# A pair's dilated attention between the half chunks of the next pair's projections, all pairs written out

## The reference, cut to what matters

```
qa, ka, va = xn @ W_in (columns by group g and head)       # 3 groups of 8 heads of 64; 2048 prompt tokens, D = 1024
for (window, dil) in ((128, 1), (512, 4), (2048, 16)):     # group g; keys at distances 0, d, 2d, ..., window
    s = q . k * 64**-0.5 + alibi bias                      # blocks of 128 queries by 256 (or 128) keys
    lse = logsumexp(s);  o = exp(s - lse) @ v
win{g}_prompt = the last min(window, 2048) rows of (k, v)  # an output
win{g}_sample = state_win{g} moved on by 4 tokens          # an output: copied DRAM to DRAM
```

## Time and profile before

| | |
|---|---|
| median of 3 runs | 3882.95 us |
| the profiled execution's own time | 3883.4 us |
| its span | 3880.7 us |
| TensorE busy | 3412.9 us, 88% |
| VectorE, ScalarE busy | 1313.1 us, 952.7 us |
| dilated stage, first projection to last value matmul | 200.24 to 1630.27 us |
| mean granted TensorE clock | 0.913 of full speed |

### The profile page before, as it was taken

How to read it: one execution, slowest core, us unless ns; L and a number is a source line. 1 busy time by engine, 2 the same in 40 slices (tenths; PEclk the granted TensorE clock), 3 DMA queues, 4 the chain that set the end, 5 groups by cost and what they waited for, 6 DMA issues and landing times. The chain is left out here.

```text
span 3880.7 us, 52570 instructions
## 1 busy us (share of the span) xinstructions
PE 3412.9 (88%) x18808; PEld 2853.8 (74%) x18808; DVE 1313.1 (34%) x3549; ACT 952.7 (25%) x1838; POOL 416.7 (11%) x557
## 2 busy tenths in 40 slices
PE   3899999999998898699999997899999997239799
PEld 3877777788776686599999996566766665138787
DVE  4111222211222112222211112556656554763333
ACT  4421222211221112212122222333333332011121
POOL 0000000000000000000000002222333320013200
PEclk6999999999997887799999999899999998569899
DMA  3133322233312222232223323223333331765443
GB/s 118 50 121 116 108 82 89 91 116 120 111 57 81 88 79 76 81 99 79 81 85 86 89 69 108 92 85 109 109 108 108 108 107 44 263 201 182 165 127 114
DMA packets 351647, 407.75 MB, mean 105 GB/s; under 512 B 114154, under 2 KB 307403, under 8 KB 349483
## 3 DMA queue, kind: packets, MB, share of 16 engines
q1 hardware_dynamic: 308186, 182.18, 16.7%
q0 software_dynamic: 43280, 223.22, 16.3%
HBM read 318.14 MB, written 175.19 MB: 127 GB/s over the span
## 5 line engine op out<-in xcount | busy, mean ns | idle before, releaser
L109 PE MATMUL dil_S<-all_xT_hi,dil_w_hi 128*128 128x512 f32 x1152 | 468.4, 407 | 17.6 <-DVE dil_w_lo L621 17.6
L110 PE MATMUL dil_S<-all_xT_lo,dil_w_hi 128*128 128x512 f32 x1152 | 461.6, 401 | 0.0
L111 PE MATMUL dil_S<-all_xT_hi,dil_w_lo 128*128 128x512 f32 x1152 | 460.7, 400 | 0.0
L109 PE MATMUL gate_ps<-all_xT_hi,gate_w_hi 128*128 128x416 f32 x960 | 346.7, 361 | 13.8 <-DVE gate_w_lo L1074 13.8
L111 PE MATMUL gate_ps<-all_xT_hi,gate_w_lo 128*128 128x416 f32 x960 | 338.5, 353 | 0.0
L110 PE MATMUL gate_ps<-all_xT_lo,gate_w_hi 128*128 128x416 f32 x960 | 337.7, 352 | 0.0
L2168 PE MATMUL mla_S<-mla_k,mla_q 96*128 96x512 f32 (+3 forms) x640 | 287.5, 567 | 12.9 <-ACT mla_p L1956 7.5
L2196 PE MATMUL mla_O<-mla_v,mla_pT 128*128 128x66 f32 x2176 | 270.5, 274 | 4.6 <-DVE mla_rec L2115 4.6
L109 PEld LDWEIGHTS dil_S<-all_xT_hi,dil_w_hi 128*128 128x128 f32 x1152 | 222.3, 193 | 67.4 <-DVE dil_w_lo L621 17.7
L2196 PEld LDWEIGHTS mla_O<-mla_v,mla_pT 128*128 128x128 f32 x2176 | 262.6, 195 | 8.9 <-issue 7.2
L111 PEld LDWEIGHTS dil_S<-all_xT_hi,dil_w_lo 128*128 128x128 f32 x1152 | 220.8, 192 | 51.7
(11 more groups left out here) (269 smaller groups left out, 5435.5 us busy)
## 6 DMA issues: line engine op xcount, KB each, us to landing
out_win_sample<-in_state_win POOLq DMA_DIRECT2D x16, 4088.0 KB, 14.7
mla_kv<-in_state_win POOLq DMA_DIRECT2D x72, 512.0 KB, 12.4
scr_gates<-gate_out POOLq DMA_DIRECT2D x120, 208.0 KB, 2.2
mla_qb<-scr_hs POOLq DMA_DIRECT2D x32, 768.0 KB, 11.8
dil_raw<-in_w_in SPq DMA_DIRECT2D x36, 512.0 KB, 4.1
proj_gm<-scr_gates SPq DMA_DIRECT2D x40, 416.0 KB, 3.3
gate_ckv<-in_cache_ckv SPq DMA_DIRECT2D x256, 64.0 KB, 1.8
out_win_sample<-in_state_win POOLq DMA_DIRECT2D x4, 4064.0 KB, 2.3
```

The costliest lines, as they stand in the source:

```text
L109: pe.matmul(out, w[0], x[0], start=first, stop=False)
L110: pe.matmul(out, w[0], x[1], start=False, stop=False)
L111: return pe.matmul(out, w[1], x[0], start=False, stop=last)
```

## The change: what it does, and the diff

Time of a pair is cut into 24 slots, one for each half chunk (12 matmuls) of its projections, written out for 12 pairs and a 13th pass without projections. In pass `n`, TensorE does the half chunk of pair n, and behind it a piece of the attention of pair a = n - 1: in an even slot 2u turns(u-1) and scores(u), in an odd slot 2u+3 values(u); slots 18 to 23 hold no attention. Projections go through a PSUM tile `PJ` of two banks; `S`, `O` and `sm` have one buffer; `raw` has one buffer instead of two, and `w` goes round by weight. V and K are transposed in slots 18 to 21. `knat` is now the two halves of `sm`. `kT` has two buffers. Record buffers stay four. GpSimd's program is the same but for blank lines. Each load of a weight waits until the one before has been split (`w_lo`), and stands in slots 4, 12 and 20 of SyncE's order.

```diff
-        raw = [m.sb(f"raw{b}", [P, KC, P]) for b in range(2)]
+        NU = NT // 2
+        NP = 4 * NG
+        raw = m.sb("raw", [P, KC, P])
...
+        knat = [sm[:, b, :, :].rearrange("p h (x c) -> p (h x) c", c=P) for b in range(2)]
+        PJ = m.ps("PJ", [P, 2, 512])
+        S = m.ps("S", [P, 2, 512])
...
+        def scored(slot):
+            return slot // 2 if slot % 2 == 0 and slot < 2 * NU else None
+        def turned(slot):
+            return slot // 2 - 1 if slot % 2 == 0 and 2 <= slot <= 2 * NU else None
+        def valued(slot):
+            return (slot - 3) // 2 if slot % 2 == 1 and 3 <= slot < 2 * NU + 3 else None
...
+                def load(p):
+                    n, o = divmod(p, 3)
+                    if p:
+                        sp.wait_ge(w_lo, p)
...
+                for n in range(NP + 1):
+                    for slot in range(SLOTS):
+                        if n < NP:
+                            p = n * 3 + slot // 8 + 2
+                            if slot % 8 == 4 and p < 3 * NP:
+                                load(p)
+                            if slot == 16:
+                                sp.wait_ge(masked, n * NU)
...
+                            if slot in (6, 14):
+                                store_sample(n, slot // 8)
+                            if TURN_FROM < slot <= TURN_FROM + KN[n // 4]:
+                                store_keys(n, slot - TURN_FROM - 1)
+                            if slot == SLOTS - 1:
+                                store_values(n)
+                                store_sample(n, 2)
+                        if n and valued(slot - 1) is not None:
+                            store_records(n - 1, valued(slot - 1))
...
+                        if n and scored(slot - 1) is not None:
+                            exps(n - 1, scored(slot - 1))
+                        if n and turned(slot) is not None:
+                            turn_out(n - 1, turned(slot))
...
+                        p = n * 3 + slot // 8 + 1
+                        if slot % 8 == 3 and 1 < p < 3 * NP:
+                            high(p)
...
-                        held(dve, rec_stored[u % 4], (n * (NU // 4) + u // 4) * 32, dve_ticks)
...
+                    if u == 0:
+                        dve.wait_ge(bias_in, a * 16 + 16)
+                        for b in range(2):
+                            dve.wait_ge(kn_stored[b], 16 * ((KN_BASE[a + 1] + 1 - b) // 2))
+                    if c > 3:
+                        dve.wait_ge(rec_stored[u % 4], c // 4 * 32)
...
+                        if n and turned(slot) is not None:
+                            turn_out(n - 1, turned(slot))
+                        if n and scored(slot) is not None:
+                            mask(n - 1, scored(slot))
+                        if n and valued(slot) is not None:
+                            record(n - 1, valued(slot))
...
+                for n in range(NP + 1):
+                    for slot in range(SLOTS):
+                        if n < NP:
+                            project(n, slot)
+                            if slot in (4, 12):
+                                sample(n, slot // 8)
...
+                        if n:
+                            if turned(slot) is not None:
+                                turns(n - 1, turned(slot))
+                            if scored(slot) is not None:
+                                scores(n - 1, scored(slot))
+                            if valued(slot) is not None:
+                                values(n - 1, valued(slot))
```

More of the change, by code:

```diff
@@ L425, in stage_dilated @@
         kn_ready, kn_out = m.sem("kn_ready"), m.sem("kn_out")
-        kn_stored = [m.sem("kn_stored_sm"), m.sem("kn_stored_raw")]
+        kn_stored = [m.sem(f"kn_stored{b}") for b in range(2)]
         v_stored, hs_stored = m.sem("v_stored"), m.sem("hs_stored")
@@ L431, in stage_dilated @@
         rec_stored = [m.sem(f"rec_stored{b}") for b in range(4)]
-        sp_ticks, dve_ticks = m.sem("sp_ticks"), m.sem("dve_ticks")
-        NU = NT // 2
         KN_TILES = [min(w_, SEQ) // P for w_, _ in GROUPS]
         KN = [-(-n // 4) for n in KN_TILES]
[L436 to L458, removed]
+        KN_BASE = [sum(KN[i // 4] for i in range(n)) for n in range(NP + 1)]
+        ORDER = (2, 1, 0)
+        READY = (vT_ready, k_ready, q_ready)
+        OUT = (vT_out, k_out, q_out)
+        SLOTS = 24
+        TURN_FROM = 18
         def blocks(g, u):
@@ L499, in body @@
                             .then_inc(v_stored, 16)
[L500 to L527, removed]
+                def store_keys(n, k):
+                    g, hp = divmod(n, 4)
+                    i = KN_BASE[n] + k
+                    tiles = min(4, KN_TILES[g])
+                    rows = slice(k * 4 * P, (k * 4 + tiles) * P)
+                    sp.wait_ge(kn_out, i + 1)
+                    sp.dma_start(t[f"win{g}_prompt"][0][rows, 0, hp * P:(hp + 1) * P].rearrange("(s p) c -> p s c", p=P),
+                                 knat[i % 2][:, 0:tiles, :]).then_inc(kn_stored[i % 2], 16)
@@ L570, in _ @@
[L570 to L612, removed]
@@ new lines, in _ @@
+                low(0)
+                low(1)
+                for n in range(NP + 1):
+                    for slot in range(SLOTS):
+                        if n and turned(slot) is not None:
[4 more added lines that the diff above has]
+                            record(n - 1, valued(slot))
+                        if n == NP:
+                            continue
+                        if slot % 2 and slot // 8 == 1:
+                            empty(n, slot % 8 // 2)
+                        if TURN_FROM <= slot < TURN_FROM + KN[n // 4]:
+                            lay_keys(n, slot - TURN_FROM)
+                        p = n * 3 + slot // 8 + 1
+                        if slot % 8 == 3 and 1 < p < 3 * NP:
+                            low(p)
@@ L796, in sample, with project @@
-                def sample(n, o):
-                    which, b = ORDER[o]
-                    if o == 0:
-                        waits(pe, rec_out, n * NU)
-                    out = O[0:NS, 0, :, :].rearrange("p a b -> p (a b)")[:, which * P:(which + 1) * P]
+                def project(n, slot):
+                    o, k, half = slot // 8, slot % 8 // 2, slot % 2
+                    p = n * 3 + o
+                    if k == 0 and half == 0:
+                        pe.wait_ge(w_lo, p + 1)
+                    if half == 0 and (n or slot > 2):
+                        n1, s1 = (n, slot - 4) if slot >= 4 else (n - 1, slot + SLOTS - 4)
+                        pe.wait_ge(OUT[s1 // 8], n1 * 4 + s1 % 8 // 2 + 1)
+                    for c in range(4 * half, 4 * half + 4):
+                        last = split_matmul(pe, PJ[:, k % 2, :], [w_hi_t[p % 2][:, c, :], w_lo_t[p % 2][:, c, :]],
+                                            [xT[x][:, c, k * 512:(k + 1) * 512] for x in range(2)], c == 0, c == KC - 1)
+                    if half:
+                        last.then_inc(READY[o], 1)
@@ L805, in sample, with turn_values @@
                     last.then_inc(hs_ready, 1)
-                each_pair(pe, body)
+                def turn_values(n, k):
+                    if k == 0:
+                        pe.wait_ge(vT_out, 4 * (n + 1))
+                        pe.wait_ge(hs_out, n * 3 + 2)
+                    else:
+                        pe.wait_ge(v_out, n * 4 + k)
+                    for s in range(4):
+                        last = pe.transpose(B[:, s, :], vT[:, tokens(n // 4, 4 * k + s)], ident[:, :])
+                    last.then_inc(v_ready, 1)
@@ new lines, in turn_keys @@
+                def turn_keys(n, k):
+                    g = n // 4
+                    if k == 0:
+                        pe.wait_ge(k_out, 4 * (n + 1))
+                    if k < 2:
+                        waits(pe, (t_out_a, t_out_b)[k], n * NU)
+                    else:
+                        pe.wait_ge(kn_out, KN_BASE[n] + k - 1)
+                    for s in range(min(4, KN_TILES[g])):
+                        at = SEQ - KN_TILES[g] * P + (4 * k + s) * P
+                        last = pe.transpose(T[:, k % 2, s, :], kT[n % 2][:, at:at + P], ident[:, :])
+                    last.then_inc(kn_ready, 1)
@@ new lines, in scores @@
+                def scores(a, u):
+                    g, c = a // 4, a * NU + u
+                    if u == 0:
+                        pe.wait_ge(q_out, 4 * (a + 1))
+                        pe.wait_ge(k_out, 4 * (a + 1))
+                    waits(pe, masked, c)
+                    for s, j, j0, nk in blocks(g, u):
+                        for h in range(2):
+                            r = slice(h * HD, (h + 1) * HD)
+                            last = pe.matmul(S[:, h, s * 2 * P:(s * 2 + nk) * P], qT[r, tokens(g, j)],
+                                             kT[a % 2][r, tokens(g, j0, nk)], start=True, stop=True)
```

(27 more changed lines are left out.)

318 lines of the change are left out of this document (131 added, 187 removed).

## The result

| | before | after |
|---|---|---|
| median | 3882.45 us | 3908.39 us (3906.08 to 3914.89, 4 runs) |
| ratio, 95% interval | | 1.0066 (1.0049 to 1.0084) |
| span of the profiled run | 3880.7 us | 3904.5 us |
| last value matmul of the dilated stage ends | 1630.3 us | 1653.7 us |
| TensorE busy | 3412.9 us | 3358.6 us |

The change makes the kernel 0.66% slower, 26 us where 40 were forecast. The dilated stage ends 23.4 us later and the profiled span is 23.8 us longer, so all but 0.4 us of it lies in the stage. TensorE does its work in 54 us less busy time and still finishes later.

What follows compares the result with a forecast made beforehand. TensorE was taken to bound the dilated stage. Passes of 75.2, 4 x 105.2, 3 x 109.2, 157.8, 446.4 and 43.5 us end it at 1671.5 instead of 1630.3, so 3883 + 40 = 3923 us; range 3840 to 3975.

Steps and rivals of the forecast that it cites:

- new wait of mask(4): Passes 8 to 11: VectorE's mask waits for unit 0's record store, stalling TensorE 42 us once and 49 us three times.
- One for one: On the large copy's two DMA engines, each small q1 packet waits for one large q0 packet, 2.4 us.
- rival A: Passes 8 to 11: small record stores get through between large packets, so no stall; 3718 us, chance 0.17.
- The pace: Passes 0 to 7 at TensorE's full clock: 75.2 us for pass 0, 105.2 with group 0, 109.2 with group 1.
- the pieces of attention: Attention work on TensorE in a group 0 pass: 3.82 us a unit, 30.6 us a pair.
- The returns: TensorE going back to projection after attention work: 16 more a pass at 0.09 us, 1.4 us.
- Passes 8 to 11: Group 2's passes, with the stall included: 157.8 us for pass 8, 148.8 us each for the other three.
- The last pass: The 13th pass, attention of pair 11 alone with single buffers: 4.8 to 5.0 us a unit, 43.5 us.
- returns from the low clock: After each stall in passes 8 to 11, TensorE runs at half clock for a while: about 2.5 us each.

Runs made afterwards that it cites:

- Experiments 1: GpSimd's large two-batch copies cut into one-batch copies: 3712.31 us (0.9549) in the changed kernel, 3801.07 us (0.9788) in the kernel before.
- 2: Changed kernel with five record buffers instead of four: 3868.39 us (0.9958); with three: 3937.92 us (1.0144).
- Experiment 5: Changed kernel with GpSimd's copies of passes 8 to 11 started at the fourth V chunk instead of the first: 3901.8 us, ratio 1.0049.
- experiment 3: Changed kernel with record stores of pairs 7 to 10 sent from an unchanging tile, no mask waiting for them: 3846.05 us, ratio 0.99.

## Why the prediction was right

- **What decides.** The forecast was "slower", by a new wait of mask(4) for unit 0's record store, held by the two-batch copy on two engines. Experiments 1 (how the copy is spread decides, not its bytes) and 2 (the count of record buffers sets where TensorE stops) show it. Stalls of 42 and three of 49 us were forecast; 41.6, 49.6, 48.1 and 48.1 came.
- **One for one.** This was taken from 26 packets against 26 and decided between the forecast and rival A. Experiment 5 shows it again for record stores, 21 against 21, on which rival A had its doubt. A's time, 3718 us, is what the kernel takes where the jam is gone: 3712, with passes of 110.2 and 96.1 us where A had 110.5 and 95.8. What the prediction gave for A by the Trainium skill (page DMA: Bandwidth & Descriptors, section Queues, rings and completion order), 7 turns and 17 us, took the page's packets of 9 to 17 descriptors for q1 alone. For both queues, as the page has it, my estimate is another: each turn of the copy would last 22 to 41 us (9 to 17 x 2.4), q1 would get 2 to 4 turns while the copy's 32 large packets per engine pass, some 35 of the 80 descriptors that it needs, and the stalls would have stayed. So the page didn't speak for A, and 3718 us doesn't follow from it.
- **The pace.** Forecast for pass 0 75.2, with group 0 105.2, with group 1 109.2; measured, from first matmul to first matmul, 75.2, 103.6 (104.0 in pass 4) and 108.9. Pass 8 began 6.5 us earlier than forecast (1017.3 for 1023.8). Nearly all of it comes from group 0: added up from start to start in pass 2, the pieces of attention take 28.8 us where I took 30.6. The returns were right: a half chunk behind a piece of attention takes 2.87 to 2.90 us, 0.09 to 0.12 more than 2.78.
- **Passes 8 to 11.** Forecast 157.8 and three of 148.8; measured 153.4, 147.7, 146.5 and 146.8, about 10 us less in all. First projection matmuls of passes 8 to 11, and the last one of pass 11:
```profile
1017.33 0.39 PE L109 MATMUL dil_PJ<-all_xT_hi,dil_w_hi 128*128 128x512 f32 x1
...
1170.70 0.39 PE L109 MATMUL dil_PJ<-all_xT_hi,dil_w_hi 128*128 128x512 f32 x1
...
1318.41 0.39 PE L109 MATMUL dil_PJ<-all_xT_hi,dil_w_hi 128*128 128x512 f32 x1
...
1464.92 0.39 PE L109 MATMUL dil_PJ<-all_xT_hi,dil_w_hi 128*128 128x512 f32 x1
...
1611.35 0.40 PE L111 MATMUL dil_PJ<-all_xT_hi,dil_w_lo 128*128 128x512 f32 x1
```
  In pass 8 the mask's release came 82.8 us after `vT_ready` (the first V chunk's last matmul ends at 1024.95), where I took 83. TensorE resumed 1.3 us earlier than forecast, and from there to the next pass's `vT_ready` it took 67.1 us instead of 70.1 (63.5 and the 6.6 of slots 0 and 1).
- **The last pass.** Forecast 4.8 to 5.0 us a unit and 43.5 in all; measured 4.84 and 41.9.
- Together the stage's end was forecast 18 us too late (1671.5 for 1653.7): the passes erred by under 4%, none of them to the other side, and so the loss is 26 us instead of 40. It is the small difference of a gain and a loss, each over 160 us. That it came within 15 us and kept its sign is partly luck; such a sum doesn't allow one to count on it.
- **Where I put nothing,** nothing came: TensorE is busy without a gap in passes 1 to 7, so masks and exponentials hide behind half chunks, and so do the copies of 4088 KB (15.1 us to landing). Written-out code brought 141 instruction packets of q8 instead of 107 over the whole kernel, and no gap.
- **Not seen ahead:** that SyncE itself stands in its issue (17.1, 19.3, 9.6 and 19.1 us in pass 8). I take it that this did no harm of its own, since what it had left to issue would have been stuck anyway; no run tests it. Nor that the copy of 992 KB lies on two more engines for the first 20 us. It was over some 60 us before the mask's release.

## What to carry to other kernels

Before work is moved, look not only at what its engine waits for but at what the transfers of the moved work will share a queue's time with: in the kernel before, group 2's record stores came when the large copy was over (SyncE was free of it at 1215.0, the second transposes came at 1225.36), and interleaving put them into it. In both kernels here a DMA copy whose outermost dimension is 2 was a jam for every transfer that needed its two engines. Cut such a copy by that dimension, and compare the wait at the first buffer that comes round again with the length of any jam. And a jam has a queue of waits behind it: taking out the one that is named (experiment 3) gives back only the distance to the next.

## What the runs showed of the hardware that was not expected

- Four copies of one batch (two of 2032 and two of 496 KB) are over in 18 us, two of two batches (4064 and 992 KB) in 80: the same bytes at less than a fourth of the pace, with 2 of 16 engines at work for the last 58 us. The Trainium skill, page DMA: Bandwidth & Descriptors, section Why a DMA increments its semaphore by 16 and not by 1, says that the number of engines is the largest up to 16 that divides, on both sides of the copy, the slowest dimension that isn't 1; a count of 2 gives 2, and these traces agree for each copy (13.0% of 16 engines is 2.1; 26.1%, or 4.2, while both run).
- The same page, section Queues, rings and completion order, has an engine drain some 9 to 17 descriptors of one ring before it turns; here q0 and q1 took turns one packet of the profile each (26 and 26, 21 and 21), and the small ones waited 2.4 us apiece. These traces don't agree with the page, and the measurement decides.
- The queue held up its issuer early: with a load and the first record store in it, SyncE stood 17.1 us over the next issue, and 35.16 us over a load behind the V store in the kernel before.
- The clock takes little. The granted clock behind the gap of pass 8:
```profile
1110.00:1115.00 5.00, 4.30 (x16) 2.92 (x17) 1.39 (x5) 1.03 (x3) 0.00 (x0) 0.50 0.09 27
1115.00:1125.00 10.00, 10.00 (x72) 8.62 (x72) 3.65 (x12) 3.40 (x7) 0.00 (x0) 0.95 0.19 50
```
  It is 0.50 (1.2 GHz) and then nearly full. The stage is 195.4 us longer with the jam than without (1453.1 against 1257.7, first to last matmul), and the gaps are 187.4 of it. So four returns from the low clock cost at most the other 8 us, 2.0 each, where the prediction took 2.5.
